# Layer 0's in-projection taken in left and right model columns, with the shift row added by TensorE

## What is computed

```python
mod = silu(c) @ w_ada[l] + b_ada[l]                 # 6 rows of 1024: sh1, sc1, g1, sh2, sc2, g2
h = rmsnorm(x, norm1_g[l]) * (1.0 + sc1) + sh1
z = h @ w_in[l]                                     # 2560 columns: u_a, v_a, q_b, k_b, v_b
out_a = gmlp_mixer(u_a, v_a, ...)                   # gelu, norm of v, 128x128 triangular mixing
out_b = diff_attention(q_b, k_b, v_b, ...)          # 4 heads, two causal softmax maps each
x = x + g1 * (concat(out_a, out_b) @ w_out[l])      # then a feed-forward stage, then layer 1 (8 experts)
```

## Time and profile before

| | before |
|---|---|
| time, median of 3 runs | 1267.23 us (1266.34 to 1270.11) |
| the profiled execution's own time | 1267.54 us |
| its span in the trace | 1264.7 us |
| PE / PEld / DVE / ACT / POOL busy | 97% / 68% / 86% / 66% / 4% |
| granted TensorE clock, mean | 0.996 |
| HBM traffic | 409.6 MB, mean 324 GB/s |

### The profile page before, as it was taken

The page is one execution under the profiler, slowest core; times in us unless marked ns, Lnnn a source line. Parts: engine busy times, 40 slices in busy tenths (PEclk is TensorE's granted clock), DMA queues, the critical chain, the costliest instruction groups (busy, mean ns, idle before and its releaser), DMA issues.

```text
span 1264.7 us, 17151 instructions
## 1 busy us (share of the span) xinstructions
PE 1223.6 (97%) x5381; PEld 857.1 (68%) x5381; DVE 1083.1 (86%) x1312; ACT 836.7 (66%) x1093; POOL 54.0 (4%) x71
## 2 busy tenths in 40 slices
PE   6999999999989998999999999999999999999996
PEld 2445767777767776776776776776776776776764
DVE  4677898788889878998998998998998998998997
ACT  3125554444465658777777777777777777777884
POOL 2102100000000202000000000000000000000000
PEclk9999999999999998999999999999999999999999
DMA  9998758898859346999999999999999999999970
GB/s 351 354 387 289 254 190 298 280 329 290 316 197 321 131 166 243 385 388 355 386 389 344 385 389 344 386 389 347 384 389 342 386 389 351 385 388 347 397 279 33
DMA packets 195950, 409.59 MB, mean 324 GB/s; under 512 B 6676, under 2 KB 45596, under 8 KB 195652
## 3 DMA queue, kind: packets, MB, share of 16 engines
q1 hardware_dynamic: 191812, 393.82, 85.4%
q0 software_dynamic: 4096, 15.25, 3.7%
HBM read 401.70 MB, written 7.34 MB: 323 GB/s over the span
## 4 chain that ended last, share of the span: by engine, by line
PE 82%; DVE 11%; ACT 3%; issue 3%; DMA 1%; SPq 1%; DVEq 0%; ACTq 0%
PE bank L2018 21%; PE bank L2019 21%; PE bank L2020 21%; PE bank L2179 5%; DVE w_lo L1333 3%; PE bank L2025 3%; PE bank L2029 2%; PE bank L2026 2%; DVE ada_acc L1385 2%; DVE more_lo L1333 1%; DMA raw<-in_w_ada 1%; PE bank L2512 1%; PE bank L2056 1%; ACT more_hi L855 1%; ACT w_hi L855 1%
## 5 line engine op out<-in xcount | busy, mean ns | idle before, releaser
L1333 DVE TENSOR_TENSOR w_lo<-raw,w_hi 128x1024 fp32r<-128x1024 f32 x366 | 441.1, 1225 | 62.9 <-ACT w_hi L855 60.7
L855 ACT ACTIVATE w_hi<-raw 128x1024 fp32r<-128x1024 f32 x366 | 383.2, 1058 | 131.8 <-PE bank L2020 115.9
L1333 DVE TENSOR_TENSOR more_lo<-raw,more_hi 128x1024 fp32r<-128x1024 f32 x264 | 315.3, 1220 | 14.0 <-ACT more_hi L855 13.4
L855 ACT ACTIVATE more_hi<-raw 128x1024 fp32r<-128x1024 f32 x264 | 276.5, 1062 | 59.6 <-PE bank L2020 59.6
L2018 PE MATMUL bank<-w_hi,hgT_hi 128*96 128x512 f32 x352 | 140.2, 398 | 0.3 <-DVE w_lo L1333 0.3
L2019 PE MATMUL bank<-w_hi,hgT_lo 128*96 128x512 f32 x352 | 139.1, 395 | 0.0
L2020 PE MATMUL bank<-w_lo,hgT_hi 128*96 128x512 f32 x352 | 138.0, 392 | 0.0
L1385 DVE SCALAR_TENSOR_TENSOR ada_acc<-raw,silu_c,ada_acc 128x512 f32<-128x512 f32 x152 | 114.7, 755 | 18.1 <-DMA raw<-in_w_ada 11.2
L2018 PE MATMUL bank<-more_hi,hgT_hi 128*96 128x512 f32 x320 | 127.1, 397 | 0.6 <-DVE more_lo L1333 0.6
L2019 PE MATMUL bank<-more_hi,hgT_lo 128*96 128x512 f32 x320 | 126.4, 395 | 0.0
L2020 PE MATMUL bank<-more_lo,hgT_hi 128*96 128x512 f32 x320 | 125.4, 392 | 0.0
(11 more groups left out here) (334 smaller groups left out, 1761.9 us busy)
## 6 DMA issues: line engine op xcount, KB each, us to landing
raw<-in_moe_w_gate SPq DMA_DIRECT2D x88, 1024.0 KB, 8.6
raw<-in_moe_w_up SPq DMA_DIRECT2D x88, 1024.0 KB, 9.0
raw<-in_moe_w_down SPq DMA_DIRECT2D x88, 1024.0 KB, 9.8
raw<-in_w_ada SPq DMA_DIRECT2D x48, 1024.0 KB, 10.8
raw<-in_w_in SPq DMA_DIRECT2D x20, 1024.0 KB, 11.6
raw<-in_ffn_w_gate SPq DMA_DIRECT2D x11, 1024.0 KB, 5.4
raw<-in_ffn_w_up SPq DMA_DIRECT2D x11, 1024.0 KB, 8.0
raw<-in_ffn_w_down SPq DMA_DIRECT2D x11, 1024.0 KB, 11.1
```

Of the source, the lines that this page charges most:

```text
L855: act.activation(like(hi_of(s)), src, ACT.Copy).then_inc(hi_done, 1)
L1333: dve.tensor_tensor(like(lo_of(s)), src, like(hi_of(s).bitcast(F32)), ALU.subtract).then_inc(split_done, 1)
```

## The change

The first six model-column quarters are taken in another order, and the shift is added in another place:

- **The list of chunks** now begins: left scale (2 chunks), left shift (2), left rows of q, right scale (2), left rows of k, right shift (2), right rows of q, M0 (2), right rows of k, then M1's and later chunks and the other `in` chunks in turn. The list has as many chunks as before; of M1 to M4 the first three are one place later than before, M4's two are last. x is loaded behind the second chunk, the gain behind the fourth.
- **Pieces 0 to 7** are q left (2), k left (2), q right (2), k right (2) (`IN_PIECES`); a fourth bank is used for the second tile of k.
- **Left blocks** are still shared by PE and DVE; of the right scale and shift DVE now does all four row tiles of both chunks, and PE only the sum (`ada_right`).
- **The shift**: POOL's and DVE's additions are gone. DVE makes x times 1/rms times scale (`row_times`); PE turns it with a product against the identity in place of a transpose (`first_turned`) and adds the shift row in the same bank with a product of the shift block against one column of the identity, read 128 times (`first_shifted`). ACT instead of DVE writes the shift blocks to `mod`.
- **POOL** starts its loads (mixing matrices, lambda rows and others) when both halves of tile 0 of `h_tok` are made, instead of after its first addition.
- **The sums** of M0, M1 and M2 stand ahead of pieces 9, 11 and 15. DVE's loop does M0 in its places 4 and 5, M1 in 6 to 9, M2 in 10 to 13, M3 in 14 to 17, and both chunks of M4 in 18 and 19.

```diff
+IN_PIECES = [[(0, 0), (0, 1), (1, 0), (1, 1), (0, 2), (0, 3), (1, 2), (1, 3)]
+             + [(t, sub) for t in range(2, 5) for sub in range(4)],
+             [(t, sub) for t in range(5) for sub in range(4)]]
+BESIDE_FIRST = [[], [], [(0, 0), (0, 1)], [(1, 0)], [(1, 1)], [(2, 0)], [(2, 1)], [(3, 0)], [(3, 1)], [(4, 0), (4, 1)]]
+FIRST_DONE = [3, 4, 6, 8, 10]
+FIRST_SUMS = {9: 0, 11: 0, 15: 2}
+FIRST_NEXT = (7, 11, 13, 16)
...
-    s = [("ada", 0, j, half) for j in FIRST_ADA for half in range(2)]
+    s = [("ada", 0, j, half) for j in FIRST_ADA[:2] for half in range(2)]
+    for step in range(2):
+        s.append(("in", 0, IN_ORDER[step], 0))
+        s += [("ada", 0, FIRST_ADA[2 + step], half) for half in range(2)]
+    for piece in range(4, 20, 2):
+        t, sub = IN_PIECES[0][piece]
+        s.append(("in", 0, IN_ORDER[t], sub // 2))
+        s += [("ada", *BESIDE_IN[0][b], half) for b, half in BESIDE_FIRST[piece // 2]]
...
             pool.wait_ge(consts, 4)
-            shift_h(0, h_tok, SH1, (0,))
+            pool.wait_ge(h_done, 2)
...
+            ada_half(0, (2, 3))
+            ada_half(1, (2, 3))
+            ada_half(0, (2, 3))
+            modulation_out(1)
+            ada_half(1, (2, 3))
+            row_times(0, 0, 0, SC1, h_tok)
+            row_times(0, 1, 0, SC1, h_tok)
             transposed(0, 0)
-            modulation_out()
+            ada_half(0)
+            ada_half(1)
+            modulation_out(3)
+            row_times(0, 0, 1, SC1, h_tok)
+            row_times(0, 1, 1, SC1, h_tok)
+            ada_half(0)
+            ada_half(1)
...
+            def first_turned(half):
+
+                for a in range(NT):
+                    wait_rows(pe, (h_done, h_own), 0, a, half)
+                    for k in range(4):
+                        c0 = P * (4 * half + k)
+                        pe.matmul(tr_bank(0, half, a)[:, P * k:P * k + P], h_tok[:, a, c0:c0 + P], ident[:, :],
+                                  start=(k == 0), stop=False, skip_group_check=True)
+
+            def first_shifted(half):
+
+                pe.wait_ge(ada_out, 2 * half + 2)
+                for a in range(NT):
+                    for k in range(4):
+                        c0 = P * (4 * half + k)
+                        last = pe.matmul(tr_bank(0, half, a)[:, P * k:P * k + P], mod[:, SH1, c0:c0 + P],
+                                         ident[:, 0:1].to_broadcast([P, P]), start=False, stop=(k == 3),
+                                         skip_group_check=True)
+                    last.then_inc(tr_mm, 1)
...
-                    t, sub = piece // 4, piece % 4
-                    if layer == 0 and sub == 1 and t in (1, 2, 3):
-                        pe.wait_ge((q_out, k_out, v_out)[t - 1], NT)
+                    t, sub = IN_PIECES[layer][piece]
+                    if layer == 0 and piece in FIRST_SUMS:
+                        pe.wait_ge((q_out, k_out, v_out)[FIRST_SUMS[piece]], NT)
                         ada_sum()
...
                     if layer == 0:
-                        if piece in (0, 2):
-                            pe.wait_ge(tr_hi, 2 + sub)
-                            pe.wait_ge(tr_lo, 2 + sub)
-                        if piece == 1:
-                            h_transposes(0, 0, 1)
-                    if piece == 3:
+                        if piece == 2:
+                            ada_right(2)
+                        if piece == 3:
+                            first_turned(1)
+                        if piece == 4:
+                            ada_right(3)
+                            first_shifted(1)
+                    if piece == (3 if layer else 6):
                         mixer_turned()
```

More of the change, by code:

```diff
@@ L388, in tr_bank @@
                 return bank[4 + 2 * a + half]
-            return bank[2 + a] if half == 0 else bank[4 + a]
+            return bank[4 + a]
         def wait_rows(engine, sems, stage, a, half):
@@ L949, in modulation_next, with shift_out @@
                     bias(i + 2)
-            def beside(i, piece):
-                if i == 0 and piece == 2:
-                    transposed(0, 1)
+            def shift_out(i):
+                act.wait_ge(ada_mm, i + 1)
+                act.wait_ge(ada_out, i)
+                act.activation(mod_block(i), sum_bank(i)[:, :], ACT.Copy).then_inc(ada_out, 1)
             def transposed(i, half):
@@ L1083, in _ @@
                             ada_no[0] += 1
+                    if layer == 0 and piece in FIRST_NEXT:
+                        modulation_next()
                     if piece == 6:
@@ L1112, in _ @@
                         in_hi(layer, piece)
-                    beside(3 * layer, piece)
                 head_out(0)
@@ L1374, in ada_half @@
                 acc = ada_acc[:, i % 2, :]
-                start = 2 if i < 4 else 0
+                start = 2 if i < 2 else 0
                 if half == 0 and tiles[0] == start:
@@ L1398, in ada_half, with last_norm @@
                     ada_no[0] += 1
-            def norm(i, a_piece, b_piece, dst, quarters=range(4)):
-                order = BY_HALF if a_piece is not None else BY_TILE
-                for n in quarters:
-                    a, half = order[n]
+            def last_norm(i, dst):
+                for a, half in BY_TILE:
                     if half == 0:
@@ L1423, in tile_lo, with row_times @@
                                   ALU.subtract).then_inc(tr_lo, 1)
+            def row_times(i, a, half, piece, dst):
+                if half == 0:
+                    dve.wait_ge(std_done, NT * i + a + 1)
+                    then(dve.reciprocal(rstd[:, a:a + 1], std[:, a:a + 1]))
+                cols = slice(CB * half, CB * half + CB)
+                dve.scalar_tensor_tensor(out=dst[:, a, cols], in0=x[:, a, cols], scalar=rstd[:, a:a + 1],
+                                         in1=mod[:, piece, cols], op0=ALU.mult, op1=ALU.mult)\
+                   .then_inc((h_done, h_own)[a], 1)
             def row_scaled(i, n, a, half, piece, dst):
@@ L1615, in _ @@
                         in_lo(layer, piece)
-                    beside(3 * layer, piece)
                     m = piece // 2 - layer
-                    if layer and piece < 4:
+                    if layer == 0:
+                        for b, part in BESIDE_FIRST[piece // 2]:
+                            if len(BESIDE_FIRST[piece // 2]) == 1:
+                                ada_half(part, (2 * q, 2 * q + 1))
+                            elif part == q:
+                                ada_half(part)
+                    elif piece < 4:
                         if piece == 3:
@@ L1622, in _ @@
                         ada_half(m % 2, (2 * q, 2 * q + 1))
[L1623 to L1624 removed]
                     if piece == 7:
+                        if layer == 0:
+                            lambda_dots()
                         mixer_rows()
@@ L2036, in ada_first @@
                 dst = bank[7 - i % 2][:, :]
-                if half == 0 and i >= 2:
-                    pe.wait_ge(ada_out, i - 1)
                 n = WHERE[("ada", *ADA[i], half)]
@@ L2090, in turned @@
                         c0 = 2 * GW + NH * DV * part + DV * h
-                        last = pe.transpose(qk_bank(part, a)[:, P * h:P * h + P], z[:, a, c0:c0 + DV], ident[:, :])
+                        last = pe.transpose(qk_bank(layer, part, a)[:, P * h:P * h + P], z[:, a, c0:c0 + DV], ident[:, :])
                     last.then_inc(qk_mm, 1)
@@ L2098, in _ @@
             pe.wait_ge(silu_b_done, 1)
-            for n in range(4):
+            for n in range(2):
                 for half in range(2):
-                    if (n, half) == (3, 1):
-                        h_transposes(0, 0, 0)
                     ada_first(n, half)
+            first_turned(0)
+            first_shifted(0)
             for layer in range(DEPTH):
@@ L2160, in bank_free @@
                         pe.wait_ge(done[t - 2], NT * (layer + 1))
-                    if a == 1 and t >= 1:
+                    if a == 1 and t >= (1 if layer else 2):
                         pe.wait_ge(done[t - 1], NT * layer + 1)
```

108 lines of the change are left out of this document (46 added, 62 removed).

## The result

The changed kernel takes 1272.87 us (median of 7 runs, 1271.99 to 1280.89) where the kernel before takes 1267.43 in the same measurement: ratio 1.0047, interval 1.0034 to 1.0060. That is slower by 5.4 us, more than a measurement of this kernel leaves open. The forecast was 1268.5, 1.3 us slower; the time lies just inside the upper end of its range (1273.0). The profiled execution has a span of 1271.0 us (before 1264.7), and 1.84 us of its time lie around it (before 2.84).

What follows compares the result with a forecast made beforehand. PE was taken to bound this stage, the weight stream close behind. A lead of 4.1 us, less 2.4, 2.0 and 1.0, gave 1.3 us slower: 1268.5 us, range 1263.1 to 1273.0.

Steps and rivals of the forecast that it cites:

- The lead: How much earlier PE starts the scores than the kernel before: 4.1 us, used up by later stalls.
- Step 2: From piece 4 up to the scores: they start at 71.3 us, 4.1 earlier, with chunk 18 landing at 67.3.
- the tail: Behind piece 16 up to the sum of M3: PE loses about 1.0 us.
- Step 5: Behind piece 16: DVE's 8 tiles of M4 delay the last map's copy, and PE loses about 1.0 us.
- the sum of M3 after 125 us: Sign at the stage's end that the prediction is wrong; it put this sum about 1.3 us later than 121.77.
- Step 3: Piece 12: PE stalls 2.4 us for DVE's copy of v, where there was no stall before.
- Step 4: Piece 16: PE stalls 2.0 us for DVE's copy of g; the piece ends at 107.9 us.
- The rival in which the lead survives: DVE keeps up at pieces 12 and 16: 3.1 to 4.1 us faster, 1264.1 or 1263.1; chance 0.2, whole or part.
- Step 1: The head, an earlier start: first piece at 26.2 us, piece 4 at 47.0, a lead of one piece.
- The slow head: Slower products after PE's early pauses: pieces 0 and 1 last 4.6 us longer, scores at 75.8, time 1273; chance 0.08.
- The two cancel: Behind the scores: M1's sum adds 0.86 us, PE's wait for the write of M2, about as much, goes.
- the worse tail: M4's 8 tiles and the maps run at DVE's slower rate, last map's copy 2 us later: 1271; chance 0.12.

Runs made afterwards that it cites:

- products in two pauses: Changed kernel plus PE products nobody reads, 7 ahead of the left shift's sum, 8 ahead of the last head's values: 1272.72 us, ratio 1.0037.

## Why the prediction was wrong

The direction was right, and Steps 3 and 4 held. The lead (Step 2) was put too high and the tail (Step 5) far too low, and so the kernel is 5.4 us slower where 1.3 was forecast. One of the prediction's own signs of being wrong came true: the sum of M3 after 125 us.

- **Step 3 and Step 4 held.** 2.4 and 2.0 us were forecast for the waits behind the copies of v and g, 2.28 and 1.70 measured, and moving the sums took each away. The rival in which the lead survives named its condition, M1's sum ahead of piece 10; the run that met it was 4.4 us (by the second measurement 2.9) faster than the change, and still 1.5 slower than the kernel before, since the waits in piece 16 and in the tail stayed.
- **Step 1** has the first piece at 26.2 and piece 4 at 47.0; it was 27.5 and 48.4 at the lower clock. At a full clock it holds: with both sums moved and M4 back the first piece starts at 26.14 and piece 4 at 47.02. The slow head was a rival with the right row in mind (pause, then slower products), but its price, all else alike 1273, was wrong: the low clock ended with the turning, so the first piece only started 1.35 us later, where this rival had two pieces 4.6 longer, and of that 0.2 to 1.2 reached the scores. That the time lies near this rival's 1273 is luck, since most of the loss is in the tail.
- **Step 2 failed by 1.35 us.** The scores at 71.3 rested on chunk 18 at 67.3, the middle between two neighbours. In the nine traces in which DVE waited for that chunk it landed at 67.0 to 68.6, in seven of them at 67.9 or later; where it landed at 67.34, the scores did come at 71.40. Why it mostly comes later there than the old order's neighbours would have it is not settled. The lead was 2.75, not 4.1. The Trainium skill (DMA: Bandwidth & Descriptors, Specifications) gives about 358 GB/s as a core's share of HBM, which the prediction set aside. The stretches of the changed kernel show 387 GB/s at 22 to 26 us and again from 50 to 68 us, so the stream is not held at that share; at 40 to 50 us it moved 310 (349 before).
- **Step 5 failed most.** It counts DVE's list down to the last map's copy and lets PE wait for that: 1.0 us. That term was about right: with ACT's copy of head 2 out of the way, the tail takes 15.18 us (103.54 to 118.72), 1.1 more than before. What the step put at nothing is who else waits for DVE's sums of the gates, which are 5.5 us later (120.11 against 114.61): ACT's roots, and behind these in ACT's list the copy of head 2. From the end of piece 16 to the sum of M3 it took 14.08 us before (107.69 to 121.77) and now 18.58 (109.39 to 127.97): 4.5 more where 1.0 was forecast. At a full clock, in the trace of M1's sum, it is 16.89 (105.99 to 122.88), 2.8 over 14.08: the wait of 2.17 for ACT and some 0.6 of small stops around it. The other 1.7 is the lower clock behind that wait, for which the step had no term either. The step named who waits for DVE on PE and didn't look at ACT's list.
- **"The two cancel" held.** M1's sum adds 0.86. M2's sum, the scores of head 2 and pieces 13 and 14 took 10.41 us before, with PE's wait for the write of M2 in them (88.52 to 98.93), and 9.56 now (89.27 to 98.83). What no step had is 0.6 around the two waits in the loop: pieces 11 and 12 take 9.50 (79.77 to 89.27), that is 7.22 without the wait, where two pieces took 6.90 before, and piece 16 in the same way 3.70 where it took 3.44.

The sum in the trace: 2.75 of lead, less 2.28, 1.70, 0.6 and 4.5, is 6.3 later; 6.36 was measured at the sum of M3. The time rose by less, 5.4, since 1.0 us less lies around the span of the profiled execution; why that is so is open. The chance of 0.17 for a slower kernel was given mainly to the head; the worse tail was priced by DVE's rate alone, at 1271, which the prediction itself took to be told only in part from no change.

## What to carry to other kernels

When a step moves later on one engine, list every engine that waits for it and what is queued behind each of those waits: here a late sum on PE held DVE's copies, and a late sum on DVE held ACT's roots, whose queue held PE. A block's reduction belongs ahead of long work on the engine that does it when another engine's queue stands still for it; moving two sums made 5.7 to 7.2 us here, of which up to 1.7 is the fuller clock behind the tail's wait in the traces. An order's parts (where a sum stands, where a block's chunks stand) have to be tried together, since M4's place alone is worth nothing with the sums late and 3 us with them early.

## What the hardware showed

**Equal pauses, unequal clocks.** Pauses of 1.90 to 1.93 us in the head were followed by a granted clock of 0.57 in both traces of the changed kernel and by 1.00 in those with M1's sum ahead of piece 10, though PE's instructions up to there are the same. The tail's 2.17 was followed by 0.79 at 122 to 130 us in both of the former and by 1.00 in both traces of the latter:

```profile
22.00:26.00 4.00, 4.00 (x34) 3.70 (x33) 0.96 (x3) 1.19 (x2) 0.00 (x0) 1.00 1.05 387
122.00:130.00 8.00, 8.00 (x37) 5.93 (x36) 5.04 (x10) 6.08 (x12) 0.00 (x0) 1.00 0.72 256
```

(M1's sum ahead of piece 10, first trace.) Over all traces with the head's code unchanged, the clock behind the head's pause was low in the three with M1's sum behind the scores (the changed kernel twice, M4 put back alone) and full in the five with it ahead; behind the tail's 2.17 it was low in four of four and full in three of three by the same division. Why the place of a later sum should go with the clock behind an earlier pause no run here shows. The wait of 2.28 in piece 12, on the other hand, was followed by 1.98 us for four records in the changed kernel and by 3.53 in the run with products in two pauses. The Trainium skill (TensorE: Matmul & The Clock Gate, What's actually happening) says that the gate's watch on the array runs on by itself and doesn't begin anew with the kernel; unequal answers to equal pauses agree with that, the likeness of two traces of one kernel is not explained by it, and no run here separates the two. The time goes with the clock between executions too: 12 runs of the kernel with M1's sum moved go from 1267.13 us at a mean granted clock of 0.997 to 1271.55 and 1271.67 at 0.993: 0.35% of the time for 0.4% of the clock. A pause of PE of some 2 us thus costs its length and, in some executions, up to 1.7 us more behind it.
